# The delta-rule block's first part: mask ahead of the exponential, one z buffer, solver blocks on two queues, and x asked for first

## The chip, the cores and the metric

The kernel runs on one core of a Trainium2 chip. The metric is device time in microseconds (us), the median of several runs. The core's engines run side by side and meet at semaphores: TensorE (PE, matrix products), VectorE (DVE), ScalarE (ACT), GpSimd (POOL), and SyncE (SP), which here only issues DMA transfers.

## The reference: what is computed

A decoder block over 512 tokens of width 1024, float32. First a mixer (gated DeltaNet beside a short gated convolution), then a top-4-of-32 mixture of experts. The part that matters here, cut down:

```python
proj = rms_norm(x) @ w_in                       # q,k,v | z | a,b | short convolution | gates
q, k = l2_normalize(q), l2_normalize(k)         # 8 heads of 128, after a causal convolution and silu
gcum = cumsum(g)                                # log decay, g <= 0, per token and head
diff = gcum[..., :, None] - gcum[..., None, :]
decay = where(causal, exp(where(causal, diff, 0.0)), 0.0)
Lm = where(strict, (beta * k) @ k.T * decay, 0.0)
T = triangular_solve(Lm + eye, eye)             # unit lower triangular inverse
u, w = T @ (v * beta), T @ (k * beta * exp(gcum))
aqk = (q @ k.T) * decay
...                                             # a scan over chunks carries the state
o = rms_norm(o, g) * silu(z)
```

## The kernel before

Every large product is made in three float32r passes: a weight tile of 128 x 4 x 512 (one *half*, `kq` 0 or 1, four row blocks k of the eight) is loaded, ScalarE copies it to a rounded `hi`, VectorE subtracts to get `lo`, and TensorE multiplies hi x hi, hi x lo and lo x hi. All orders are written out by hand, one instruction stream for each engine, and the program is cut into blocks; at the end of a block every engine waits for all the others. Three places are touched.

**The front** (block of L189). SP asks for the convolution taps and gains (L197, three small transfers that land in `small_rows`), then x in four tiles of 128 tokens (L200, 512 KB each), then weights (L207). ScalarE sums squares (L257), VectorE scales the rows (L370), TensorE turns x (L466) into PSUM, ScalarE writes `xT_hi` (L267) and VectorE `xT_lo` (L376). VectorE makes the first weight half's `lo` (L384) before the first `xT_lo`. TensorE's first group (`group`, L482 to L484) needs `lo` of the half and four tiles of `xT_lo` before its first product.

**The first part of the delta-rule block** (block of L616, names from L590 on), for four chunks c of 128 tokens, 8 heads, in two halves g of four heads. TensorE turns k (L824), VectorE gets its squared norms (L735). The running decay `gc` comes from a product with the triangular mask `tri` (L867 to L869); its rows go to DRAM and come back broadcast over the partitions into `aqkT` (L635). VectorE subtracts `gc` per head and clips at 0 (`differences`, L741, 8 per chunk), ScalarE exponentiates (`exps`, L686), GpSimd multiplies with the causal mask (L661), and then multiplies the rows beta over norm, which came back broadcast in `LT` (L641), with that decay (L666). TensorE makes the q k and k k products of a chunk (`products`, L837; each shows as 2 records, 16 for a chunk), VectorE multiplies them into `LT` (L754) and `aqkT` (L756). The diagonal 32 x 32 blocks of `LT` go to DRAM (`blocks_out`, L627, 4 transfers per chunk) and return in one transfer as `W` (L649), one block per partition; VectorE inverts all 128 at once in 60 dependent small steps (L799 to L805), and the result goes to DRAM (L651).

Beside this runs the z projection, two groups of 192/2 = 96 products (L855 to L857): `zraw` (L621) to `zhi` on ScalarE (L691), to `zlo` on VectorE (`z_low`, L746), to TensorE, and its output through silu into `zT` (`z_out`, L697). TensorE's order is

```python
                products(0)
                z(0, (0, 1))
                products(1)
                z(0, (2,))
                products(2)
                z(0, (3,))
                products(3)
                z(0, (4, 5, 6, 7))
                z(1, range(KD))
```

where `products(c)` waits until VectorE has read the banks of chunk c - 1 (semaphore `s_AT`, set by L756).

**The second part** (block of L928). SP brings the inverses of chunk 0 back as the diagonal of `U` (L935) once GpSimd has zeroed it (L959); GpSimd also masks `LT` into `M` (L948). TensorE turns q and v, turns U (all L1136) and multiplies (L1130); ScalarE copies between them (L988, L994, L1011, L1000).

## Time and profile before

| | us |
|---|---|
| median of 3 runs | 1955.07 (1954.26 to 1959.21) |
| the profiled execution's own time | 1953.42 |
| its span in the trace | 1951.5 |
| PE busy | 1837.3 (94%) |
| DVE busy | 1492.9 (77%) |
| ACT busy | 1106.7 (57%) |
| POOL busy | 409.4 (21%) |
| mean granted TensorE clock | 0.969 |

The span is what the trace covers. The device time of the same execution is 1.9 us longer; the rest lies before the first and after the last instruction. All positions below are us from the span's start. The front is 0 to about 20, the first part of the delta-rule block 293.5 to 386.4, its second part follows to about 480, and the experts fill the rest. PE's busy time counts overlapping matmuls, so the distance from start to start is what one costs.

### The profile page before, as it was taken

The page shows a single profiled execution, that of the slowest core. Times are in us where ns is not written, and L with a number is a line of the kernel's source. Part 1 is how long each engine was busy: PE and PEld are TensorE (multiplying, and loading weights), DVE is VectorE, ACT ScalarE, POOL GpSimd, SP SyncE. Part 2 cuts the span into 40 slices and gives each one's busy share as a digit, 9 for nine tenths or more (in the row PEclk, how much of TensorE's full clock was granted, in tenths as well). Part 3 has the DMA queues.
Part 4 walks back from the last instruction along what each step waited for, and adds up shares of the span by engine and source line. Part 5 has one row for each costly group of instructions (what it writes and reads, how often), then busy time and mean ns, then how long its engine had stood idle before and what let it go on. Part 6 is the DMA issues. An engine that isn't in the chain of part 4 may idle for free.

```text
span 1951.5 us, 24205 instructions
## 1 busy us (share of the span) xinstructions
PE 1837.3 (94%) x8612; PEld 1529.0 (78%) x8612; DVE 1492.9 (77%) x1107; ACT 1106.7 (57%) x890; POOL 409.4 (21%) x337
## 2 busy tenths in 40 slices
PE   7999997897999985899999999999999999999995
PEld 6888875796888874688888888888888888888883
DVE  4336567657233546889999999999999999999996
ACT  4123443243241232677777777777777777777772
POOL 0000006052000010532132222322322223223231
PEclk9999997998999986999999999999999999999998
DMA  4322225102562244879999999999999999999985
GB/s 154 108 87 86 86 87 179 30 10 77 204 237 87 87 146 180 314 297 373 383 353 384 378 354 383 358 374 384 347 382 371 360 384 356 373 381 347 382 321 231
DMA packets 129070, 508.06 MB, mean 260 GB/s; under 512 B 25572, under 2 KB 25764, under 8 KB 94917
## 3 DMA queue, kind: packets, MB, share of 16 engines
q1 hardware_dynamic: 119780, 490.96, 66.0%
q0 software_dynamic: 9248, 16.54, 2.3%
q8 instruction: 28, 0.46, 0.1%
...
## 4 chain that ended last, share of the span: by engine, by line
PE 56%; DMA 1%; POOL 1%; DVE 1%; issue 1%; ACT 1%; SPq 0%; POOLq 0%; ACTq 0%; DVEq 0%
PE PM L2118 12%; PE PM L2117 12%; PE PM L2120 12%; PE PM L2136 6%; PE PM L2137 6%; PE PM L2139 6%; PE PM L2097 2%; PE PM L2111 2%; PE PM L2103 1%; DMA xg<-xn_scratch,now 1%; DMA mraw<-expert_rows_scratch 1%; DVE zT L2065 0%; POOL put_back L1923 0%; DVE zT L2073 0%; POOL by_weight L1921 0%
## 5 line engine op out<-in xcount | busy, mean ns | idle before, releaser
L1624 DVE TENSOR_TENSOR mlo<-mraw,mhi 128x2048 fp32r<-128x2048 f32 x384 | 907.5, 2397 | 60.1 <-ACT mhi L1620 58.4
L1620 ACT ACTIVATE mhi<-mraw 128x2048 fp32r<-128x2048 f32 x384 | 721.9, 1914 | 115.7 <-PE PM L2120 112.6
L2117 PE MATMUL PM<-mhi,xgT_hi 128*128 128x512 f32 x1024 | 403.3, 394 | 0.0
L2118 PE MATMUL PM<-mlo,xgT_hi 128*128 128x512 f32 x1024 | 400.5, 391 | 0.0
L2120 PE MATMUL PM<-mhi,xgT_lo 128*128 128x512 f32 x1024 | 273.9, 389 | 0.0
L2117 PEld LDWEIGHTS PM<-mhi,xgT_hi 128*128 128x128 f32 x1024 | 193.3, 189 | 40.1
L2118 PEld LDWEIGHTS PM<-mlo,xgT_hi 128*128 128x128 f32 x1024 | 193.2, 189 | 39.9
L2120 PEld LDWEIGHTS PM<-mhi,xgT_lo 128*128 128x128 f32 x1024 | 192.3, 188 | 40.5
L2136 PE MATMUL PM<-mhi,hT_hi 128*128 128x512 f32 x512 | 202.7, 396 | 1.1 <-DVE hT_lo L2034 1.1
L2137 PE MATMUL PM<-mlo,hT_hi 128*128 128x512 f32 x512 | 199.9, 390 | 0.0
L1895 POOL TENSOR_TENSOR glu<-glu 128x1024 f32<-128x1024 f32 x32 | 76.6, 2394 | 551.0 <-DVE glu L2029 551.0
L2139 PE MATMUL PM<-mhi,hT_lo 128*128 128x512 f32 x512 | 158.2, 390 | 0.0
L384 DVE TENSOR_TENSOR lo<-raw,hi 128x2048 fp32r<-128x2048 f32 x24 | 55.0, 2292 | 123.1 <-ACT hi L275 123.1
L482 PE MATMUL PS<-xT_hi,hi 128*128 128x512 f32 x352 | 137.9, 392 | 3.7 <-DVE xT_lo L376 2.7
L1402 DVE TENSOR_TENSOR lo<-qkvT,hi 128x2048 fp32r<-128x2048 f32 x20 | 45.8, 2292 | 124.8 <-ACT hi L1339 124.8
L483 PE MATMUL PS<-xT_lo,hi 128*128 128x512 f32 x352 | 137.7, 391 | 0.0
L484 PE MATMUL PS<-xT_hi,lo 128*128 128x512 f32 x352 | 137.4, 390 | 0.0
L275 ACT ACTIVATE hi<-raw 128x2048 fp32r<-128x2048 f32 x24 | 46.0, 1916 | 121.2 <-PE PS L484 120.7
L2136 PEld LDWEIGHTS PM<-mhi,hT_hi 128*128 128x128 f32 x512 | 96.5, 188 | 20.4 <-issue 1.5
L2139 PEld LDWEIGHTS PM<-mhi,hT_lo 128*128 128x128 f32 x512 | 96.4, 188 | 20.3
L1339 ACT ACTIVATE hi<-qkvT 128x2048 fp32r<-128x2048 f32 x20 | 38.2, 1913 | 130.4 <-PE PS L1499 123.9
L2137 PEld LDWEIGHTS PM<-mlo,hT_hi 128*128 128x128 f32 x512 | 96.5, 189 | 19.0
(331 smaller groups left out, 2623.6 us busy)
## 6 DMA issues: line engine op xcount, KB each, us to landing
mraw<-in_w_gate_up_dram SPq DMA_DIRECT2D x256, 1024.0 KB, 8.2
mraw<-in_w_down_dram SPq DMA_DIRECT2D x128, 1024.0 KB, 7.7
raw<-in_w_in_dram SPq DMA_DIRECT2D x24, 1024.0 KB, 5.1
qkvT<-in_w_in_dram SPq DMA_DIRECT2D x8, 1024.0 KB, 6.4
...
mraw<-expert_rows_scratch SPq DMA_DIRECT2D x6, 1024.0 KB, 12.1
zraw<-in_w_in_dram SPq DMA_DIRECT2D x4, 1024.0 KB, 6.2
qkvT<-in_w_o_gdn_dram SPq DMA_DIRECT2D x4, 1024.0 KB, 5.7
```

The costliest lines, as they stand in the source:

```text
L482: pe.matmul(dst, w_hi, xT_hi[:, k, :], start=(k == 0), stop=False)
L483: pe.matmul(dst, w_hi, xT_lo[:, k, :], start=False, stop=False)
L484: mm = pe.matmul(dst, w_lo, xT_hi[:, k, :], start=False, stop=(k == KD - 1))
L1620: nc.scalar.activation(mhi[:, split_slot(m), :], mraw[:, raw_slot(m), :], ACT.Copy).then_inc(e_h, 1)
L1624: nc.vector.tensor_tensor(mlo[:, split_slot(m), :], mraw[:, raw_slot(m), :], mhi[:, split_slot(m), :].bitcast(F32), ALU.subtract).then_inc ...
L1895: nc.gpsimd.tensor_tensor(hid, up, sig, ALU.mult).then_inc(s_hid, 1)
L2117: pe.matmul(gate_up_bank[:, n, :], xgT_hi[:, k, :], w_hi[:, n, :], start=False, stop=False)
L2118: pe.matmul(gate_up_bank[:, n, :], xgT_hi[:, k, :], w_lo[:, n, :], start=False, stop=False)
L2120: mm = pe.matmul(gate_up_bank[:, n, :], xgT_lo[:, k, :], w_hi[:, n, :], start=False, stop=(k == KD - 1))
L2136: pe.matmul(y_bank[:, n, :], hT_hi[:, k, :], w_hi[:, kk, n, :], start=(k == 0), stop=False)
L2137: pe.matmul(y_bank[:, n, :], hT_hi[:, k, :], w_lo[:, kk, n, :], start=False, stop=False)
L2139: mm = pe.matmul(y_bank[:, n, :], hT_lo[:, k, :], w_hi[:, kk, n, :], start=False, stop=(k == KD - 1))
```

## The change

In the front, the first two tiles of x are asked for ahead of the small transfers; VectorE makes four tiles of `xT_lo` ahead of the first `lo`; TensorE's first group does its hi passes of the first half (32 products) as soon as `hi` and those four tiles are there, and its lo passes (16) behind them.

In the first part of the delta-rule block: the causal mask is applied by GpSimd ahead of the exponential, as a select that puts -1e30 where the mask is off, on the rows as they come from DRAM; the subtraction of `gc` becomes the bias of the exponential, so that ScalarE runs it per head (32 instead of 8 instructions), with `ngc` = -`gc` from a new small VectorE instruction; VectorE's `differences` are gone, and the product of the beta rows with the decay moves from GpSimd to VectorE (`decayed_gates`). `zraw` has one half instead of two, so a load of z weights waits for the `zlo` of the half before it. One k block of z comes ahead of `products(0)`, and the first z split (ScalarE's copy) moves up. The last `zlo` moves from VectorE, in the middle of the inversion, to GpSimd. Blocks go out on SP's and ScalarE's queues, two each for a chunk, and come in per chunk. The inverses go out in two transfers (32 and 96 partitions), and those of chunks 0 and 1 are brought into `U` before the block ends, `U` being zeroed at its start.

```diff
+        for t in range(2):
+            sp.dma_start(x_rows[:, t, :], x_d[:, t, :]).then_inc(s_x[t], 16)
         n = 0
         for src, rows in ((gdn_conv_w[0].rearrange("j (c p) -> (j c) p", p=P), CONV * QKV),
                           (sconv_w[0].rearrange("j (c p) -> (j c) p", p=P), SCONV * KD),
                           (norm_mix_g[0].rearrange("(c p) -> c p", p=P), KD)):
             sp.dma_start(small_rows[n:n + rows, :], src).then_inc(s_rows, 16)
             n += rows
-        for t in range(TT):
+        for t in range(2, TT):
...
+        turned(range(GT))
         split(0, [0])
-        turned(range(KD))
+        turned(range(GT, KD))
...
-            for kq in range(2):
+            first = isinstance(g, int) and g == 0
+            if first:
+                pe.wait_ge(s_h, 1)
+                pe.wait_ge(s_xl, GT)
+                for k in range(GT):
+                    for j in range(GT):
+                        w_hi = hi[:, 0, k, j * P:(j + 1) * P]
+                        pe.matmul(PS[:, j, :], w_hi, xT_hi[:, k, :], start=(k == 0), stop=False)
+                        pe.matmul(PS[:, j, :], w_hi, xT_lo[:, k, :], start=False, stop=False)
+                pe.wait_ge(s_l, 1)
+                for k in range(GT):
+                    for j in range(GT):
+                        mm = pe.matmul(PS[:, j, :], lo[:, 0, k, j * P:(j + 1) * P], xT_hi[:, k, :],
+                                       start=False, stop=False)
+                mm.then_inc(s_used, 1)
+            for kq in range(1 if first else 0, 2):
                 pe.wait_ge(s_l, 2 * g + kq + 1)
                 for kk in range(GT):
                     k = GT * kq + kk
-                    if isinstance(g, int) and g == 0:
-
-                        pe.wait_ge(s_xl, max(k + 1, GT))
+                    if first:
+                        pe.wait_ge(s_xl, k + 1)
...
+FAR_BELOW = -1e30
...
+U = p2_sb("U", [P, 2, HEADS, P])
...
-zraw = pa_sb("zraw", [P, 2, GT, GW])
+zraw = pa_sb("zraw", [P, GT, GW])
...
+def blocks_out(eng, c, bs):
+    eng.wait_ge(s_LT, 2 * c + 2)
+    for b in bs:
+        rows = slice(b * BLK, (b + 1) * BLK)
+        eng.dma_start(blocks_of(nb_d, c)[b], LT[rows, c, :, rows]).then_inc(s_nb[c], 16)
+
+def blocks_in(eng, c):
+    eng.wait_ge(s_nb[c], 16 * QB)
+    eng.dma_start(W[of_chunk(c)].rearrange("p j i -> p (j i)"), nb_d[of_chunk(c)]).then_inc(s_W, 16)
+
+def inverses_in(eng, c, bs):
+    for b in bs:
+        rows = slice(b * BLK, (b + 1) * BLK)
+        eng.dma_start(U[rows, c, :, rows], blocks_of(ub_d, c)[b]).then_inc(s_uin[c], 16)
...
+            wait(sp, z_l, 2 * zg + kq)
+            sp.dma_start(zraw[:], Z_SOURCES[zg][:, kq * GT:(kq + 1) * GT, :]).then_inc(s_zraw, 16)
...
-        load_z(0, 1)
...
-        load_z(1, 0)
-        blocks_out(0)
+        load_z(0, 1)
+        for c in CHUNKS:
+            blocks_out(sp, c, (0, 1))
+            if c >= 1:
+                blocks_in(sp, c - 1)
+            if c == 2:
+                load_z(1, 0)
+        blocks_in(sp, LAST)
         load_z(1, 1)
-        for c in range(1, TT):
-            blocks_out(c)
-        sp.wait_ge(s_nb, 16 * QB * TT)
-        sp.dma_start(W[:].rearrange("p j i -> p (j i)"), nb_d).then_inc(s_W, 16)
         sp.wait_ge(s_solved, 1)
-        sp.dma_start(ub_d, W[:].rearrange("p j i -> p (j i)")).then_inc(s_ub, 16)
+        sp.dma_start(ub_d[of_chunk(0)], W[of_chunk(0)].rearrange("p j i -> p (j i)")).then_inc(s_ub, 16)
+        sp.wait_ge(s_uz, 2)
         sp.wait_ge(s_ub, 16)
+        inverses_in(sp, 0, (0, 1))
+        sp.wait_ge(s_ubr, 16)
+        inverses_in(sp, 1, range(QB))
+        for c in range(2):
+            sp.wait_ge(s_uin[c], 16 * QB)
...
+        for c in range(2):
+            nc.gpsimd.memset(U[:, c], 0.0).then_inc(s_uz, 1)
         for c in CHUNKS:
             for g in BOTH:
-                pool.wait_ge(s_exp, 2 * c + g + 1)
-                nc.gpsimd.tensor_tensor(half(aqkT[:, c], g), half(aqkT[:, c], g), each(tri[:]),
-                                        ALU.mult).then_inc(s_tri, 1)
-            for g in BOTH:
-                pool.wait_ge(s_bin[c], 16)
-                pool.wait_ge(s_tri, 2 * c + g + 1)
-                nc.gpsimd.tensor_tensor(half(LT[:, c], g), half(LT[:, c], g), half(aqkT[:, c], g),
-                                        ALU.mult).then_inc(s_decL, 1)
+                pool.wait_ge(s_gin[c], 16)
+                nc.gpsimd.affine_select(out=half(aqkT[:, c], g), in_=half(aqkT[:, c], g), compare_op=ALU.is_ge,
+                                        fill=FAR_BELOW, base=0, pattern=[[0, HS], [1, P]], channel_multiplier=-1
+                                        ).then_inc(s_tri, 1)
         pool.wait_ge(s_redk, 2 * TT + 1)
         pool.wait_ge(s_ones, 2)
         nc.gpsimd.tensor_tensor(rk, ssk, minus_half[:], ALU.pow).then_inc(s_rk, 1)
+        pool.wait_ge(z_h, 4)
+        nc.gpsimd.tensor_tensor(zlo[:, 1, :, :], zraw[:], zhi[:, 1, :, :].bitcast(F32), ALU.subtract).then_inc(z_l, 1)
...
         def exps(c):
             for g in BOTH:
-                act.wait_ge(s_diff, HEADS * c + HS * g + HS)
-                nc.scalar.activation(half(aqkT[:, c], g), half(aqkT[:, c], g), ACT.Exp).then_inc(s_exp, 1)
+                act.wait_ge(s_tri, 2 * c + g + 1)
+                for h in range(HS * g, HS * (g + 1)):
+                    n = c * HEADS + h
+                    ins = nc.scalar.activation(aqkT[:, c, h, :], aqkT[:, c, h, :], ACT.Exp, bias=ngc[:, n:n + 1])
+                ins.then_inc(s_exp, 1)
...
+        z_hi(0, 0)
         squares(2)
         squares(3)
         by_token(2)
-        z_hi(0, 0)
-        act.wait_ge(s_gc, 3)
+        act.wait_ge(s_gc, 4)
         nc.scalar.activation(eg, gc, ACT.Exp).then_inc(s_small, 1)
         nc.scalar.activation(egl, egl, ACT.Exp).then_inc(s_small, 1)
         nc.scalar.activation(ekd, ekd, ACT.Exp).then_inc(s_small, 1)
-        exps(0)
-        exps(1)
-        z_hi(0, 1)
-        exps(2)
-        exps(3)
+        for c in CHUNKS:
+            exps(c)
+        for c in CHUNKS:
+            blocks_out(act, c, (2, 3))
+            if c == 0:
+                z_hi(0, 1)
         z_hi(1, 0)
         z_out(0)
         z_hi(1, 1)
+        act.wait_ge(s_solved, 1)
+        act.dma_start(ub_d[HB:], W[HB:].rearrange("p j i -> p (j i)")).then_inc(s_ubr, 16)
+        act.wait_ge(s_uz, 2)
+        act.wait_ge(s_ub, 16)
+        inverses_in(act, 0, (2, 3))
...
-        def differences(c):
-            dve.wait_ge(s_gin[c], 16)
-            for h in range(HEADS):
-                row = aqkT[:, c, h, :]
-                nc.vector.tensor_scalar(row, row, gc[:, c * HEADS + h:c * HEADS + h + 1], 0.0, ALU.subtract,
-                                        ALU.min).then_inc(s_diff, 1)
+        def decayed_gates(c):
+            dve.wait_ge(s_bin[c], 16)
+            for g in BOTH:
+                dve.wait_ge(s_exp, 2 * c + g + 1)
+                nc.vector.tensor_tensor(half(LT[:, c], g), half(LT[:, c], g), half(aqkT[:, c], g),
+                                        ALU.mult).then_inc(s_decL, 1)
...
+        nc.vector.tensor_scalar(ngc, PB[:, 7, 0, 0:TH], -1.0, None, ALU.mult).then_inc(s_gc, 1)
...
-        dve.wait_ge(s_gc, 3)
-        differences(0)
         dve.wait_ge(s_browT, 1)
         nc.vector.tensor_copy(row_sb[:, 1, :], PB[0:TH, 0, 0, :]).then_inc(s_brs, 1)
-        differences(1)
         z_low(0, 0)
-        differences(2)
-        differences(3)
-        products(0)
-        z_low(0, 1)
-        products(1)
-        products(2)
+        for c in CHUNKS:
+            decayed_gates(c)
+            products(c)
+            if c == 1:
+                z_low(0, 1)
         z_low(1, 0)
-        products(3)
         dve.wait_ge(s_brow, 1)
         dve.wait_ge(s_small, 3)
         nc.vector.scalar_tensor_tensor(out=ebk, in0=brow, scalar=-1.0, in1=eg, op0=ALU.mult,
                                        op1=ALU.mult).then_inc(s_brk, 1)
-        dve.wait_ge(s_W, 16)
+        dve.wait_ge(s_W, 16 * TT)
...
-                z_low(1, 1)
...
+        z(0, (0,))
         products(0)
-        z(0, (0, 1))
+        z(0, (1,))
...
-        for c in CHUNKS:
+        for c in range(2, TT):
...
-        clear(0)
         masks(0)
-        clear(1)
```

How TensorE's order moves in the first part of the delta-rule block (L875 and L920 turn the beta rows; L837 and L882 are `products`; L855 to L857 and L900 to L902 are z). Before:

```order
L875 MATMUL PB<-ident,by_tok 32x128
L837 MATMUL PB<-qkvT 128x256 x8
L855 MATMUL PB<-xT_hi,zhi 128x512
L856 MATMUL PB<-xT_lo,zhi 128x512
L857 MATMUL PB<-xT_hi,zlo 128x512
```

With the change:

```order
L920 MATMUL PB<-ident,by_tok 32x128
L900 MATMUL PB<-xT_hi,zhi 128x512
L901 MATMUL PB<-xT_lo,zhi 128x512
L902 MATMUL PB<-xT_hi,zlo 128x512
L900 MATMUL PB<-xT_hi,zhi 128x512
```

The twelve products of one k block of z stand between the turned beta rows and `products(0)` now; before, 24 stood between `products(0)` and `products(1)`, and now there are twelve.

VectorE's order from the row `brow` (beta over norm) on, through the first two chunks. Before:

```order
L778 SCALAR_TENSOR_TENSOR by_tok<-by_tok 128x32
L741 TENSOR_SCALAR aqkT<-aqkT,by_tok 128x128 x8
L783 COPY row_sb<-PB 32x128
L741 TENSOR_SCALAR aqkT<-aqkT,by_tok 128x128 x8
L746 TENSOR_TENSOR zlo<-zraw,zhi 128x2048
L741 TENSOR_SCALAR aqkT<-aqkT,by_tok 128x128 x16
L754 TENSOR_TENSOR LT<-PB,LT 128x512
L756 TENSOR_TENSOR aqkT<-PB,aqkT 128x512
```

With the change:

```order
L829 SCALAR_TENSOR_TENSOR by_tok<-by_tok 128x32
L832 COPY row_sb<-PB 32x128
L796 TENSOR_TENSOR zlo<-zraw,zhi 128x2048
L791 TENSOR_TENSOR LT<-LT,aqkT 128x512 x2
L804 TENSOR_TENSOR LT<-PB,LT 128x512
L806 TENSOR_TENSOR aqkT<-PB,aqkT 128x512
```

The 32 differences have left VectorE, the copy of the beta rows stands eight instructions earlier, and two products LT x decay stand ahead of each chunk's four products with PSUM.

GpSimd's order in the same block. Before:

```order
L661 TENSOR_TENSOR aqkT<-aqkT,tri 128x512 x2
L666 TENSOR_TENSOR LT<-LT,aqkT 128x512 x2
L661 TENSOR_TENSOR aqkT<-aqkT,tri 128x512 x2
L666 TENSOR_TENSOR LT<-LT,aqkT 128x512 x2
L670 TENSOR_TENSOR by_tok<-by_tok,minus_half 128x32
```

With the change:

```order
L700 MEMSET U 128x1024 x2
L704 AFFINE_SELECT aqkT<-aqkT 128x512 x8
L709 TENSOR_TENSOR by_tok<-by_tok,minus_half 128x32
L711 TENSOR_TENSOR zlo<-zraw,zhi 128x2048
L985 UNCONDITIONAL_BRANCH
```

Sixteen two-input products have become eight one-input selects, and the last `zlo` comes behind the power (L670, now L709).

## Rows read from the trace of the kernel before

**Rows 1.** The page: busy us by engine.
```profile
PE 1837.3 (94%) x8612; PEld 1529.0 (78%) x8612; DVE 1492.9 (77%) x1107; ACT 1106.7 (57%) x890; POOL 409.4 (21%) x337
```

**Rows 2.** Timeline, front: start, us, engine, line, operation, count [idle before, releaser].
```profile
0.80 0.40 SPq L197 DMA_DIRECT2D qkvT<-in_gdn_conv_w_dram  x1
...
2.04 1.78 SPq L200 DMA_DIRECT2D qkvT<-in_x_dram  x4
...
5.36 1.06 ACT L257 ACTIVATE qkvT<-qkvT 128x1024 f32<-128x1024 f32 x1 [3.29 <-DMA qkvT<-in_x_dram]
...
16.06 4.73 ACT L267 ACTIVATE xT_hi<-PS,cols 128x512 fp32r<-128x512 f32 x8 [1.69 <-PE PS L466]
...
19.66 0.71 PE L482 MATMUL PS<-xT_hi,hi 128*128 128x512 f32 x1 [2.67 <-DVE xT_lo L376]
```

**Rows 3.** Timeline of POOL, first part of the delta-rule block, and one front row.
```profile
2.83 0.29 POOL L233 TENSOR_SCALAR_AFFINE_SELECT tri<-tri 128x128 f32<-128x128 f32 x1
...
313.90 2.58 POOL L666 TENSOR_TENSOR LT<-LT,aqkT 128x512 f32<-128x512 f32 x2 [0.29 <-DMA LT<-beta_rows_scratch]
...
326.28 1.26 POOL L661 TENSOR_TENSOR aqkT<-aqkT,tri 128x512 f32<-128x512 f32 x1
...
329.77 4.54 POOL L666 TENSOR_TENSOR LT<-LT,aqkT 128x512 f32<-128x512 f32 x2
334.27 5.46 POOL L670 TENSOR_TENSOR by_tok<-by_tok,minus_half 128x32 f32<-128x32 f32 x1
```

**Rows 4.** Timeline of DVE, same block.
```profile
305.62 1.66 DVE L741 TENSOR_SCALAR aqkT<-aqkT,by_tok 128x128 f32<-128x128 f32 x8 [0.35 <-DMA aqkT<-decay_rows_scratch]
307.19 0.27 DVE L783 COPY row_sb<-PB 32x128 f32<-32x128 f32 x1
...
311.16 16.65 DVE L741 TENSOR_SCALAR aqkT<-aqkT,by_tok 128x128 f32<-128x128 f32 x16
...
330.13 3.05 DVE L746 TENSOR_TENSOR zlo<-zraw,zhi 128x2048 fp32r<-128x2048 f32 x1
...
356.44 0.09 DVE L799 MEMSET W<- 128x32 f32 x1 [5.59 <-DMA W<-blocks_scratch]
...
363.18 2.29 DVE L746 TENSOR_TENSOR zlo<-zraw,zhi 128x2048 fp32r<-128x2048 f32 x1
```

**Rows 5.** Timeline of PE, same block.
```profile
307.61 6.48 PE L837 MATMUL PB<-qkvT 128*128 128x256 f32 x16 [2.00 <-DVE row_sb L783]
...
329.06 6.01 PE L837 MATMUL PB<-qkvT 128*128 128x256 f32 x16 [9.49 <-DVE aqkT L756]
```

**Rows 6.** Timeline of PE, same block, later.
```profile
337.68 3.61 PE L837 MATMUL PB<-qkvT 128*128 128x256 f32 x16
```

**Rows 7.** Windows: length, busy of PE, PEld, DVE, ACT, POOL, granted clock, DMA, GB/s.
```profile
329.00:334.20 5.20, 5.14 (x13) 4.19 (x14) 5.20 (x6) 0.00 (x0) 5.20 (x3) 0.54 0.17 25
...
360.60:384.30 23.70, 23.63 (x96) 19.07 (x96) 18.64 (x49) 1.68 (x2) 0.00 (x0) 0.93 0.06 23
```

**Rows 8.** DMA issues, 285 to 400: KB each, median us to landing.
```profile
zraw<-in_w_in_dram SPq DMA_DIRECT2D x4, 1024.0 KB, 6.2
...
W<-blocks_scratch SPq DMA_DIRECT2D x1, 512.0 KB, 3.2
inverses_scratch<-W SPq DMA_DIRECT2D x1, 512.0 KB, 2.7
U<-inverses_scratch SPq DMA_DIRECT2D x8, 32.0 KB, 1.9
```

**Rows 9.** Timeline of all engines where the block ends and the next begins.
```profile
380.90 0.34 SPq L651 DMA_DIRECT2D inverses_scratch<-W  x1
...
384.29 2.06 ACT L697 ACTIVATE zT<-PB 128x512 f32<-128x512 f32 x4 [22.02 <-PE PB L857]
...
391.33 1.59 PE L1136 MATMUL PB<-ident,U 128*128 128x128 f32 x8 [2.74 <-DMA U<-inverses_scratch]
...
393.45 2.17 ACT L1011 ACTIVATE vb<-PB,by_tok 128x128 f32<-128x128 f32 x8
```

37 lines of the change are left out of this document (16 added, 21 removed).

## The prediction

> **What bounds the kernel now.** I read the page first: PE is busy 94% of the span [rows 1]. So a microsecond is won only where PE stands idle or runs at the lower clock, and I looked for those places with the waits of PE, then with the timelines of the stretches around them. Three lie inside the change: the front, the first part of the delta-rule block (293.5 to 386.4), and the first microseconds of its second part. Everything behind shifts as a whole: the expert part waits for its own data and not for a fixed time.
>
> The front [rows 2]: the first square starts at 5.36, when x lands, and x was asked for at 2.04, behind three small transfers that began at 0.80. PE's first weight product comes at 19.66, released by the fourth xT_lo, whose chain is held by the turned x (xT_hi waits 1.69 for PE).
>
> The delta-rule block [rows 3 to 5]: PE makes the products of chunk 0 (307.61), then z, and then stands 9.49 us until VectorE has read chunk 0 (329.06). The reader is to see why VectorE is late. Eight differences take 1.66 while GpSimd is quiet, sixteen take 16.65 while GpSimd multiplies masks and gates [rows 4]: 0.2 against 1.04 us each. And for VectorE's zlo at 330.13, 3.05 us instead of 2.29, GpSimd's pair at 329.77 takes 4.54 instead of 2 x 1.26 [rows 3, 4]. When PE resumes, chunk 1 costs 6.01 against 3.61 for a later chunk [rows 5, 6], and the granted clock of 329.0 to 334.2 is 0.54 [rows 7]: the lower level, 1.2 GHz, after an idle PE.
>
> **Part by part.** I give times on the axis of the old trace, and add the front at the end.
>
> *Front.* x is asked for 1.24 us earlier (2.04 - 0.80). The first squares follow it; the taps now arrive behind two x tiles, but are needed only when the first variance is, after the first square. The weight half lands in the same order as before and ScalarE, which splits it, had been free for 1.69 us when the turned x came. VectorE's lo, 2.29 us, would have stood in the way of an xT_lo that starts earlier; it now comes behind four of them, and PE has 32 hi products meanwhile. A product of 128x512 takes 0.229 us from start to start at the full clock (23.63 / 96, times the mean clock of 0.93 [rows 7]), so that is over 7 us: cover enough. I take -1.1 us; bounds 0 (the weights turn out to hold it) and -1.24.
>
> *Beta rows.* The copy at 307.19 [rows 4] stood behind eight differences (1.66). These go; against that ScalarE's first z split (about 1.9 us) now precedes the last squares and delays the norms by about 1. I put the copy at 306.4. LT of chunk 0 was there at 313.90, 6.7 us after the copy [rows 3]: now about 313.1. VectorE's first zlo runs 306.7 to 309.0, and up to one select later, so PE starts z at 309.5 instead of products at 307.61: **+1.9**.
>
> *Selects and exponentials.* A select of 128x128 takes 0.29 us on GpSimd [rows 3]. The new ones have four times the columns: between 0.3 and 4 x 0.29 = 1.2 us; I take 1.2, as the memory has to be passed. Eight from 305.6, when aqkT of chunk 0 is there [rows 4], are done by 315 to 317. ScalarE's 32 exponentials with a bias per head I price by its per-head copies, 8 in 2.17 us [rows 9]: 2.2 per chunk, 8.7 in all, done by about 318. The first chunk is needed at 313, the last at about 332. Both are covered; the cover is gone when a select costs over about 3 us.
>
> *VectorE.* A product of 128x512 costs a quarter of 2.29, about 0.6 [rows 4]. Per chunk there are two with the decay and four with PSUM, 3.6 us; with two zlo that is 19 us against 4 x (3.61 + 12 x 0.229) = 25.4 us of PE between 309.5 and the end of chunk 3. The 32 differences, some 20 us (16.65 and twice 1.66), are off the engine. Chunk 0's rows are read by about 319.5, when PE is still in its second k block of z, so the 9.49 us wait goes, and with it the second start at the lower clock, 6.01 - 3.61 = 2.40. What is late next is nothing on this stretch: PE itself is. The first start at the lower clock stays as it was (6.48 for 16 records against 3.61).
>
> PE sum: -9.49 - 2.40 + 1.9 = **-10.0**. z's last silu ended at 384.29 + 2.06 = 386.35 [rows 9]; it would end at 376.35. PE's wait for the first z_out, with the lower clock behind it (0.93 in 360.6 to 384.3 [rows 7]), stays.
>
> *The inversion.* PE ends chunk 3 at 309.5 + 25.4 + 2.9 (start at the lower clock) = 337.8. Then 0.7 for LT, 0.9 for two issues, 1.9 to land, 3.2 for W at most, which was one transfer four times as large [rows 8]: solve start about 343.9 instead of 356.44. SP and ScalarE each issue two of the four now, and the z split behind ScalarE's last issues ends at about 341, its zlo at 343, so this is no later. With one zraw a load takes 6.2 us [rows 8] from its request: the third is asked for at about 333, the fourth at 343, and they are wanted at 339 and 349: just covered.
>
> The inversion lasted 380.90 - 356.44 = 24.5 us [rows 4, 9]. The zlo leaves it, -2.29. But GpSimd now runs that zlo of 128x2048 beside it, 4 x 1.26 = 5.1 us. What does VectorE pay? From both sides: 33% while they overlap (3.05 against 2.29), 1.7 us; or all 5.1. I take 5.1, because rows 3 and 4 fit whole-instruction blocking: VectorE's zlo was asked at 330.13, GpSimd's first product would end at 331.03, and 331.03 - 330.13 + 2.29 = 3.2 against 3.05; GpSimd's second then starts at 333.2, ends 334.4, and 334.31 is measured. The SBUF page of the Trainium skill (Who interferes with whom) says the same against this edit: a VectorE instruction with two SBUF inputs and a GpSimd instruction that reads SBUF exclude each other for the whole length of the first. By that rule the block ends at 377.7, by sharing at 376.35, where z holds it.
>
> So the inversion ends at 343.9 + 24.5 - 2.3 + 5.1 = 371.2. The inverses go out (2.7 at most for 96 partitions), SP issues four loads for chunk 1 (1.8), the last lands after 1.9 [rows 8]: +6.5, 377.7. That is 1.35 behind z. The block ends there: 386.35 - 377.7 = **-8.65**.
>
> *Second part.* U is there when it starts. PE's 2.74 us wait for it goes [rows 9], and the eight turned tiles behind it, 1.59 us at the lower clock, run at the full one, -0.55: **-3.3** together. The masks that GpSimd makes first (1.26 each [rows 3]) no longer stand behind the zeroing of U. Bounds -2.0 and -4.5.
>
> Sum: -1.1 - 8.65 - 3.3 = -13.05. Against the profiled execution's 1953.42 that gives 1940.4; the median of the runs is 1.65 higher, 1955.07, and gives **1942.0**.
>
> **The rivals.** *A: the new order of z on PE is hit by late neighbours.* LT is a broadcast of 512 KB per chunk that shares the queue with a z load, the power (5.46 us on GpSimd [rows 3]) now stands beside the second chunk's gates on VectorE, and the fourth z load may land late. For it: the blocking seen above; against: PE has 2.7 us of z between any two chunks. A wait of 2 us with a new start at the lower clock (2.4) costs 4.4: 1946.4. Chance 0.18.
>
> *B: more is won.* GpSimd's zlo costs the inversion little, the start of z is not held by a select, and the second part gains 4.5 as its whole first round runs at the full clock: -1.35 - 0.5 - 1.2: 1939.0. For it: PE has nothing to wait for there any more. Against: after the turned U ScalarE has eight per-head copies (2.17 us [rows 9]) in the chain, at whatever clock PE runs. Chance 0.22.
>
> *C: the gain is lost behind the inversion.* The solve chain starts no earlier than some transfer allows: the last z half or W lands 5 us late, or the z split on GpSimd runs at twice its price (the pair at 329.77 took nearly that [rows 3]), 10 us, and holds the last half of z on PE. GpSimd can start it at 351.6 (z's first group ends at 347.6, the silu and the split take 4.0) and would end at 361.6, about when PE reaches that half (48 products, 12 us, behind the wait for the silu at 350), so only the inversion pays, 5 us more: 1947.0; with transfers late as well it comes within 0.3% of no change (1949.2 or more). Chance 0.12.
>
> *D: slower.* One mechanism: the select with its two-dimensional pattern over four heads is slow on GpSimd. It is first in each chunk's chain (select, exponential, gate, product). Up to about 3.1 us each nothing is felt; the eighth is needed at about 331, after 25 us. Beyond, each microsecond costs eight. At 4.8 us each the 13 us are gone, at 6 us it is 10 us slower than before: 1965. For it: 128x512 with this pattern is not in the trace; against: 0.29 us for a quarter of it. Chance 0.03.
>
> *E: the change doesn't do what it says,* since z on PE alone holds the block: then the idle PE time would have to be filled by something else. The 9.49 us is a true stand of PE behind one named semaphore, so I give it 0.02, at 1953.
>
> **How the numbers follow.** The sum as worked out has 0.43, B 0.22, A 0.18, C 0.12, D 0.03, E 0.02. The likeliest's own bounds: front 1.2 us up or down to -1.24, copy and z start 1.5 either way, inversion path 3, second part 1.3. I let the range reach over A and B: 1935 to 1949, which leaves out most of C's tail, D and E. A measurement can tell about 0.3%, 5.9 us: faster is below 1949.2. Faster: all of the sum, A and B and half of C, 0.88; within 0.3%: 0.08; slower: 0.04.
>
> **What would show it.** In the new trace: the first weight product at about 18.5; no PE wait of more than 1 us between 309 and 337 (after the front's shift, 1.1 less each), and a granted clock of 1.0 from about 315 on; VectorE's first memset of W near 343; a VectorE wait of about 5 us inside the inversion, beside GpSimd's zlo; the last z product 10 to 11 us earlier; no U wait in the second part. The sum is wrong if the select takes over 3 us, if PE stops at the second or fourth half of z, or if the block's last act is not the return of the inverses or z's silu.

## The result and the profile after

| | before | changed |
|---|---|---|
| median of 5 runs each | 1956.86 (1954.26 to 1959.40) | 1940.77 (1937.69 to 1944.97) |
| the profiled execution's own time | 1953.42 | 1942.97 |
| its span | 1951.5 | 1941.0 |
| mean granted TensorE clock | 0.969 | 0.973 |

The ratio of the times is 0.9923, with a 95% interval of [0.991, 0.9936]; ratios below are given in the same way. The changed kernel is 0.8% faster, and the median is 1.2 us below the 1942.0 predicted. A later set of runs of the same kernel gave 0.9927 [0.9915, 0.994] (below, e12).

The page by engine answers to [rows 1]:

```profile
PE 1830.4 (94%) x8612; PEld 1523.6 (78%) x8612; DVE 1479.1 (76%) x1083; ACT 1111.3 (57%) x914; POOL 390.6 (20%) x330
```

VectorE has 24 instructions less, ScalarE 24 more. PE's busy time fell by 6.9 us with the same count. Inside the first part of the delta-rule block it is 74.7 before and 68.8 now, for 299 records each: fewer matmuls ran at the lower clock there. The total is no measure of the block, though: e3 (below), whose block is the old one, also shows 1831.7.

The waits of PE (line waited for: total, times, longest):

```profile
PE PS L463 <- DMA qkvT<-in_norm_mix_g_dram: 7.0, 1, 7.0
...
PE PB L920 <- DVE by_tok L829: 5.1, 1, 5.1
...
PE PB L1177 <- PEq L656: 3.7, 1, 3.7
...
PE PB L900 <- DVE zlo L796: 2.6, 1, 2.6
...
PE PB L900 <- ACT zT L741: 2.2, 1, 2.2
```

The 9.49 us behind VectorE's products [rows 5] is gone from the list. Inside the block there are now 5.1 for the beta rows and 2.6 for the first zlo, ahead of z, where the kernel before had 2.2 for the beta rows and 2.0 for their copy; at the end of the block 3.7 behind the return of the inverses. (In e12, a second trace of the changed kernel, the first of these is 2.5 and the last 2.4.)

VectorE through the block (timeline: start, us, engine, line, operation [idle before, releaser]), against [rows 4]:

```profile
304.89 0.28 DVE L832 COPY row_sb<-PB 32x128 f32<-32x128 f32 x1 [0.49 <-PE PB L920]
305.10 2.27 DVE L796 TENSOR_TENSOR zlo<-zraw,zhi 128x2048 fp32r<-128x2048 f32 x1
...
311.69 1.29 DVE L791 TENSOR_TENSOR LT<-LT,aqkT 128x512 f32<-128x512 f32 x2 [4.32 <-DMA LT<-beta_rows_scratch]
...
341.34 0.09 DVE L845 MEMSET W<- 128x32 f32 x1
...
350.76 4.71 DVE L849 TENSOR_TENSOR wprod<-W 128x238 f32<-128x238 f32 x1
...
355.50 0.41 DVE L851 TENSOR_TENSOR W<-W,wprod 128x238 f32<-128x238 f32 x1
```

And GpSimd, against [rows 3]:

```profile
303.73 7.07 POOL L704 TENSOR_SCALAR_AFFINE_SELECT aqkT<-aqkT 128x512 f32<-128x512 f32 x8 [9.25 <-DMA aqkT<-decay_rows_scratch]
310.77 5.46 POOL L709 TENSOR_TENSOR by_tok<-by_tok,minus_half 128x32 f32<-128x32 f32 x1
350.42 4.78 POOL L711 TENSOR_TENSOR zlo<-zraw,zhi 128x2048 fp32r<-128x2048 f32 x1 [34.19 <-ACT zhi L735]
```

GpSimd's work on the rows is over after 7 us, where it had gone on from 309 to 334. One step of the inversion takes 4.71 instead of about 0.4 us; it starts 0.34 behind the start of GpSimd's 4.78 and ends 0.27 behind its end.

Windows (length, busy of PE, PEld, DVE, ACT, POOL, granted clock, DMA, GB/s), against [rows 7]: the first 5.5 us of z, the rest of the block, and the first 4 us of the second part:

```profile
307.40:312.90 5.50, 5.48 (x13) 4.32 (x14) 1.21 (x2) 5.02 (x19) 5.50 (x7) 0.50 0.80 255
312.90:371.20 58.30, 56.05 (x245) 45.81 (x243) 42.89 (x88) 11.10 (x16) 8.11 (x2) 1.00 0.33 94
374.90:378.90 4.00, 3.97 (x23) 4.00 (x24) 1.37 (x2) 1.22 (x3) 3.99 (x4) 0.60 0.01 4
```

One start at the lower level (1.2 GHz), then 58 us of full clock (2.4 GHz) with PE busy for 56 of them. In e12 those 58 us are not all at the full level, as the part on the prediction shows.

To compare kernels I take a few landmarks from each trace, all but the first two relative to the block's start (GpSimd's memset of ones, 293.52 before): the first memset of W (solve start), the inversion's length, the end of z's last silu, GpSimd's first instruction of the second part, with which PE begins too (block end), ScalarE's first copy of turned U, and the first copy of `vnew`, some 17 us into the second part.

| | first weight product | block's start | solve start | inversion | silu end | block end | U copy | vnew |
|---|---|---|---|---|---|---|---|---|
| before | 19.66 | 293.52 | 62.92 | 24.46 | 92.83 | 93.10 | 98.59 | 115.98 |
| changed | 18.59 | 292.43 | 48.91 | 26.55 | 80.90 | 82.48 | 86.44 | 103.26 |
| e12 (changed, again) | 17.34 | 289.58 | 48.47 | 26.50 | 82.01 | 82.30 | 84.73 | 101.54 |
| e1 | 20.11 | 293.94 | 49.24 | 24.48 | 77.19 | 77.47 | 83.19 | 100.38 |
| e2 | 21.38 | 296.39 | 49.77 | 24.46 | 79.60 | 79.87 | 85.09 | 101.91 |
| e3 | 17.58 | 289.79 | 63.41 | 24.46 | 93.27 | 93.55 | 98.74 | 116.21 |
| e4 | 18.22 | 291.82 | 48.23 | 24.47 | 81.77 | 82.06 | 84.49 | 101.32 |
| e5 | 17.79 | 290.01 | 48.83 | 26.56 | 80.82 | 81.11 | 85.38 | 102.20 |
| e6 | 18.04 | 293.06 | 46.49 | 26.51 | 80.02 | 80.32 | 82.75 | 99.56 |
| e7 | 18.50 | 292.33 | 48.36 | 26.56 | 80.49 | 80.86 | 84.96 | 101.79 |
| e8 | 18.36 | 290.58 | 48.72 | 24.46 | 78.78 | 79.07 | 81.50 | 98.32 |
| e9 | 18.17 | 293.20 | 49.13 | 24.44 | 77.10 | 77.38 | 83.07 | 100.35 |
| e10 | 18.43 | 292.05 | 46.93 | 24.47 | 76.79 | 77.08 | 81.18 | 97.99 |
| e11 | 18.95 | 292.71 | 45.48 | 24.46 | 75.34 | 75.63 | 78.06 | 94.87 |

In the profiled pair `vnew` moved from 409.50 to 395.69, 13.8 us, but the end only by 10.5. The rest is scatter of the expert part: from its first gather of tokens until the experts' rows are back from DRAM the fourteen traces take 1165.9 to 1169.4, whatever the kernel; before has the shortest, the changed kernel 1168.8. One trace is therefore worth no more than some 3 us at its end, and the landmarks tell more of a single change than one time does.

The landmarks scatter too. Three pairs of traces have the same code in this block: changed and e12, e1 and e9, e10 and e11. Their block ends differ by 0.18, 0.09 and 1.45 us, their `vnew` by 1.72, 0.03 and 3.12. Single traces that differ by less than that prove nothing by themselves.

### The profile page after: what moved, and what is told of

Same layout as the page of the kernel before. It is cut to its first block, busy times and chain, and to the rows that moved or that the text cites. A ratio compares the mean times of both kernels' runs of the same rounds, so it can differ in the third digit from the quotient of the medians.

```text
span 1941.0 us, 24208 instructions
## 1 busy us (share of the span) xinstructions
PE 1830.4 (94%) x8612; PEld 1523.6 (78%) x8612; DVE 1479.1 (76%) x1083; ACT 1111.3 (57%) x914; POOL 390.6 (20%) x330
## 4 chain that ended last, share of the span: by engine, by line
PE 57%; DMA 1%; POOL 1%; DVE 1%; issue 1%; ACT 1%; SPq 0%; POOLq 0%; ACTq 0%; DVEq 0%
PE PM L2159 12%; PE PM L2158 12%; PE PM L2161 12%; PE PM L2177 6%; PE PM L2178 6%; PE PM L2180 6%; PE PM L2138 2%; PE PM L2152 2%; PE PM L2144 1%; DMA xg<-xn_scratch,now 1%; DMA mraw<-expert_rows_scratch 1%; DVE zT L2106 0%; DVE zT L2114 0%; POOL by_weight L1962 0%; ACT glu L2047 0%
## 5 line engine op out<-in xcount | busy, mean ns | idle before, releaser
L499 PE MATMUL PS<-xT_hi,hi 128*128 128x512 f32 x336 | 130.9, 390 | 1.0 <-ACT ab L299 1.0
L500 PE MATMUL PS<-xT_lo,hi 128*128 128x512 f32 x336 | 130.8, 389 | 0.0
L501 PE MATMUL PS<-xT_hi,lo 128*128 128x512 f32 x336 | 130.7, 389 | 0.0
```

Source lines behind the costliest of these rows:

```text
L499: pe.matmul(dst, w_hi, xT_hi[:, k, :], start=(k == 0), stop=False)
L500: pe.matmul(dst, w_hi, xT_lo[:, k, :], start=False, stop=False)
L501: mm = pe.matmul(dst, w_lo, xT_hi[:, k, :], start=False, stop=(k == KD - 1))
```

## The experiments

**e1, the rows alone.** The old kernel with the select on GpSimd, the exponential with a bias and the gates on VectorE; z, queues, `U` and front as before.

```diff
-pool: aqkT *= tri ; LT *= aqkT          (after s_exp, s_bin)
+pool: affine_select(aqkT, fill=FAR_BELOW)  (after s_gin)
-act:  Exp(half(aqkT))                   +act: Exp(aqkT head, bias=ngc)
-dve:  differences(0..3)                 +dve: decayed_gates(c) ahead of products(c)
```

> The kernel before with one part of the change alone: the select ahead of the exponential, the bias on ScalarE, the decay product on VectorE. Two z buffers, the old z order, one queue, the old reload of U, the old front. Theory (the gain is the end of the exclusion between GpSimd and VectorE, and with it of PE's 9.49 us stand and of the start at the lower clock behind it): no PE wait of over 1 us between products(0) and products(3), products(0) itself about 1.7 us earlier, the block's last silu 12 to 14 us earlier than 386.35, time 1943 to 1945 against 1956.9 before. Rival (the gain needs the new z order, the second queue and the early reload): less than half of it, 1950 or more, with a PE wait before products(1).

Measured: median 1939.59 of 4 runs, 0.992 [0.9899, 0.9941]. The whole gain is there with this part alone; it is more than was expected (the last silu ends at 371.13, 15.2 us earlier, and the time lies below the 1943 to 1945). VectorE's timeline in e1:

```profile
304.64 0.28 DVE L782 COPY row_sb<-PB 32x128 f32<-32x128 f32 x1 [0.48 <-PE PB L875]
...
313.82 1.29 DVE L741 TENSOR_TENSOR LT<-LT,aqkT 128x512 f32<-128x512 f32 x2 [6.43 <-DMA LT<-beta_rows_scratch]
...
343.18 0.09 DVE L799 MEMSET W<- 128x32 f32 x1 [5.52 <-DMA W<-blocks_scratch]
```

PE's waits in e1:

```profile
PE PB L875 <- DVE by_tok L779: 3.1, 1, 3.1
...
PE PB L1136 <- PEq L617: 2.4, 1, 2.4
...
PE PB L855 <- ACT zT L697: 2.2, 1, 2.2
...
PE PB L1136 <- DMA U<-inverses_scratch: 1.6, 1, 1.6
```

The block ends at 77.5 after its start, against 93.1 before and 82.4 (mean of 82.48 and 82.30) for the whole change. So inside the block the rest of the change costs 4.9 us (e9, with the same block, ends at 77.38); by the time `vnew` is made it has given 2 to 4 of them back (no wait for U), and is 1.2 to 2.9 late. The solve starts as early (49.24) with W in one transfer and the old queues as with two queues and a transfer per chunk (48.91, 48.47).

**e2, GpSimd without its mask products.** The old kernel, its causal mask on the decay left out of the computation: GpSimd's eight products with `tri` are gone, VectorE's 32 differences stay.

```diff
-nc.gpsimd.tensor_tensor(half(aqkT[:, c], g), half(aqkT[:, c], g), each(tri[:]), ALU.mult)
```

> The kernel before without GpSimd's eight multiplications by the causal mask (left out, so the decay is not masked); everything else stays. Exclusion theory: the last sixteen differences take 3 to 7 us instead of 16.65, since GpSimd's products with the beta rows only begin when those have landed (313.9), and PE's wait before products(1) falls from 9.49 to under 2 us; the last silu is 9 to 12 us earlier. Rival (VectorE's differences are slow for another reason, such as the broadcast transfers that write aqkT and LT at the same time): they still take over 12 us.

Measured: one run, 1944.31, before at 1956.07 beside it. VectorE's timeline in e2:

```profile
308.22 1.66 DVE L737 TENSOR_SCALAR aqkT<-aqkT,by_tok 128x128 f32<-128x128 f32 x8 [1.88 <-DMA aqkT<-decay_rows_scratch]
...
313.76 5.45 DVE L737 TENSOR_SCALAR aqkT<-aqkT,by_tok 128x128 f32<-128x128 f32 x16
```

Not one instruction of VectorE changed, and sixteen differences take 5.45 instead of 16.65 us [rows 4]; PE's 9.49 is gone and the solve starts at 49.77. GpSimd's first product now comes at 316.50, so most of the sixteen have no neighbour. VectorE was slow because of GpSimd's products, as the prediction read it. With all 32 differences still on VectorE the block ends 13.2 us earlier than before (79.87 against 93.10); e1, without them, has 15.6 (1.1 of the 2.4 between them is the clock behind the silu wait, see below).

**e3, the front alone,** in the old kernel (the front's part of the diff above).

> The kernel before with the changed front alone (two x tiles asked for first, four tiles of xT_lo ahead of the first lo, the hi passes of the first half ahead of its lo passes). First weight product 1.0 to 1.2 us earlier than 19.66, the delta-rule block starts 1.0 to 1.2 us earlier than 293.5, time 1 us less, which the runs can hardly tell. Rival: the taps, late behind x, hold the variance, and nothing is won.

Measured: median 1952.38 of 10 runs, 0.9981 [0.9969, 0.9993]: 1.4 to 6.1 us, 3.7 at the middle. The first weight product comes 2.1 us earlier than before and the block starts 3.7 earlier, both more than the 1.0 to 1.2 expected. The block behind it is as before (93.55). **e9, rows and front together,** asks the same from the other side:

> The kernel before with two parts of the change: the rows part of e1 and the front part of e3. By their landmarks the two are independent, so the delta-rule block takes 77 to 78 us to its second part (as in e1; 82.5 in the changed kernel) and the start moves 1 to 2 us: 1936 to 1939, that is, equal to or 1 to 4 us faster than the whole change, whose other parts (one z buffer, z ahead of the products, two queues, early reload) would then cost more than they bring. Rival (they do bring something that one trace of e1 hid): the whole change is faster than this one by 2 us or more.

Measured: 1940.16 of 5 runs, 0.9922 [0.991, 0.9935]. Beside e1 it shows nothing for the front, whose few microseconds the intervals of both cover; beside the whole change in the same set (e12, 1939.47 of 6 runs) it shows no difference either, and it missed the 1936 to 1939 expected. The rest of the change (the order of z, one `zraw`, two queues, the early return of the inverses, the last zlo on GpSimd) brings nothing that the times can tell.

**e4, the last zlo back on VectorE.**

```diff
-pool.wait_ge(z_h, 4)
-nc.gpsimd.tensor_tensor(zlo[:, 1, :, :], zraw[:], zhi[:, 1, :, :].bitcast(F32), ALU.subtract)
+if k == 14: z_low(1, 1)     # inside the inversion
```

> The changed kernel with the last zlo back on VectorE, between steps 15 and 16 of the inversion; GpSimd's is gone. Exclusion theory: the inversion takes 24.5 us instead of 26.55 (one step no longer waits 4.3 us, 2.3 us come in for the zlo); the block then ends with z's silu, 1.3 us earlier than 374.9, and PE, idle for 2.4 instead of 3.7 us, begins the second part at the full clock: 1.3 to 2.7 us in all. Rival (the slow step was no blocking but the size of its own): it stays at 4.7 us.

Measured: one run, 1938.97. VectorE's timeline in e4:

```profile
349.91 0.41 DVE L849 TENSOR_TENSOR W<-W,wprod 128x238 f32<-128x238 f32 x1
350.36 2.29 DVE L794 TENSOR_TENSOR zlo<-zraw,zhi 128x2048 fp32r<-128x2048 f32 x1
352.56 0.40 DVE L847 TENSOR_TENSOR wprod<-W 128x240 f32<-128x240 f32 x1
```

The inversion is 24.47 long, with 2.29 of zlo inside, against 26.55 with 4.71 of standing. Moving 2.29 us of work off a busy engine cost that engine 4.3, nearly twice as much. The expected 1.3 us at the block's end did not come: it ends at 82.06 with z's silu, beside 82.48 and 82.30, because TensorE's second group of z ran at the lower clock in this trace (more on that below). So the shorter inversion shows in the inversion and not in the time.

**e5, the inverses brought in late,** as before the change.

```diff
-inverses_in(sp, 0, (0, 1)); inverses_in(sp, 1, range(QB)); waits for s_uz, s_uin
-act: inverses_in(act, 0, (2, 3))
-for c in range(2, TT):      # second part's loads of U
+for c in range(TT):
```

> The changed kernel with U brought in as before, all of it in the second part, and the first part ending without it. The block then ends with z's silu, 1.3 us earlier than 374.9, but the turned U waits again 2 to 3 us: ScalarE's first copy of the turned U 0 to 2 us later than at 378.87. So the early reload is worth 2 us at most. Rival (it carries much of the gain): 4 us or more later.

Measured: one run, 1937.1; `vnew` at 102.20, between the two traces of the whole change (103.26 and 101.54). PE has no wait for U in this trace, where 2 to 3 us were expected: its sixteen turnings ran at the lower clock for 3.16 us, the transfers could start at 371.10, as `U` had been zeroed long before, and the first U is turned at 374.38. So the early return shows no gain here, and what took the wait away is at least in part the early zeroing.

**e6, products(0) ahead of z,** with the first z split left early.

```diff
-z(0, (0,)); products(0); z(0, (1,))
+products(0); z(0, (0, 1))
```

> The changed kernel with the old order on PE: products(0) straight behind the turned beta rows, then two k blocks of z. Products(0) no longer wait for the first zlo (2.57 us): they start at about 305.2 instead of z at 307.42, and the wait before products(1) stays under 1 us. z's end 1 to 2 us earlier than 371.23; the block's end is set by the inverses, whose start may move up by as much. Rival (the z block ahead of products(0) is what covers VectorE): a PE wait of several us comes back before products(1).

Measured: one run, 1940.7. PE's timeline in e6:

```profile
305.10 0.39 PE L920 MATMUL PB<-ident,by_tok 128*32 128x128 f32 x1 [5.32 <-DVE by_tok L829]
...
305.96 6.04 PE L882 MATMUL PB<-qkvT 128*128 128x256 f32 x16 [0.47 <-DVE row_sb L832]
```

In the changed kernel the place reads:

```profile
307.42 0.79 PE L900 MATMUL PB<-xT_hi,zhi 128*128 128x512 f32 x1 [2.57 <-DVE zlo L796]
```

PE begins its long run 0.47 after it has been released by the copy of the beta rows, instead of 2.57 for the zlo, and the block ends 2.1 earlier (80.32 against 82.4). The second group of z starts 53.8 us after the block's start, against 55.6 to 56.3 in all five traces with z ahead of products(0) (changed, e12, e4, e5, e7), so this is more than scatter. The 5.3 for the beta rows stays, but such a wait is no measure by itself: with the same code it is 5.1 in one trace and 2.5 in e12. The copy of the beta rows is one: it comes 12.4 to 12.9 us after the block's start in the seven traces where ScalarE's z split stands ahead of the last squares, and 10.4 to 12.1 in the four where it stands behind them (e1, e9, e10, e11).

**e7, SP's last wait gone:** the second part no longer waits at its start until U is loaded.

```diff
-for c in range(2):
-    sp.wait_ge(s_uin[c], 16 * QB)
```

> The changed kernel without SP's last wait in the first part (for the inverses of chunks 0 and 1 to have landed; TensorE waits for them itself in the second part). The block ends with z's silu: 1.3 us earlier than 374.9; PE stands 2.4 instead of 3.7 us and starts the second part at the full clock: the first copy of the turned U 1.3 to 2.8 us earlier than 378.87.

Measured: one run, 1939.24; the block ends 0.4 behind z's silu (80.49 and 80.86) instead of 1.6, 1.5 us earlier. (In e12, whose silu ends late, that distance is 0.3 with the wait in place.) PE stood 2.61 us and then did not start at the full clock, as had been expected, but at 0.57 of it for 4 us. The U copy comes at 84.96, between the two of the whole change (86.44, 84.73).

**e8, three edits at the block's end:** e4's (one step later), e7's, and z's second group in the banks that the products have left, so that it does not wait for the first group's silu.

```diff
-dst = PB[:, 4 + j]                       -pe.wait_ge(z_bank, GT * zg)
+dst = PB[:, 4 * (1 - zg) + j]            +pe.wait_ge(s_AT, 2 * TT)
-z_out(0); z_hi(1, 1)
+z_hi(1, 1); z_out(0)
```

> The changed kernel with three steps: the last zlo on VectorE in the inversion, no wait for the inverses at the block's end, and z's second group in the four banks of the products, so that it need not wait for the first group's silu (2.25 us and a dip of the clock). z's end at about 368.5 instead of 371.23, its silu ends at 370.6 instead of 373.3, ScalarE's first copy of the turned U at 373 to 375 instead of 378.87: 4 to 5.5 us in all.

Measured: one run, 1933.26 beside 1958.78 of before; the block ends at 79.07, `vnew` at 98.32, 3 to 5 earlier than in the whole change. PE does not wait between z's groups, and z ends at 76.13, against 78.80 (changed) and 79.92 (e12).

**e10, the change with five edits:** the three of e8, e6's, and the first z split back behind `by_token(2)`. Three of them undo a part of the change (e6's, the z split, the last zlo); the banks and the missing wait are new. **e12** is the change unchanged in the same set.

> The changed kernel with five edits: products(0) ahead of z, the first z split back behind the squares, the last zlo on VectorE, no wait for the inverses at the block's end, z's second group in the products' four banks. The block to its second part takes 75 to 77 us instead of 82.5, ScalarE's first copy of the turned U comes 77.5 to 79.5 us after the block's start instead of 86.4; no clock dip between z's groups. Time 1931 to 1934. Rival (the inverses' way through DRAM sets the second part's start whatever PE does): 1936 or more.

> The changed kernel once more, on the same chip and beside the others of this call: 1939 to 1942, and landmarks within the scatter of the front (first weight product 17.8 to 18.6): delta-rule block 82 to 83 us to its second part.

Measured: e10 1932.75 of 4 runs, 0.9881 [0.9867, 0.9895]; e12 1939.47 of 6, 0.9927 [0.9915, 0.994]. The intervals do not touch: e10 is 6.7 us faster than the change and 22 faster than before (1954.95 in that set). It is the fastest of the versions run (e11, below, can't be told from it). The landmarks account for a part of that: `vnew` comes at 97.99, 3.6 us earlier than in e12 (101.54) and 5.3 earlier than in the first trace of the change (103.26). Beside e9 they differ by 2.4 at `vnew`, and the medians by 7.4. Where the rest lies is open. Some is left at the block's end. ScalarE's timeline in e10:

```profile
365.82 0.86 ACTq L654 DMA_DIRECT2D U<-inverses_scratch  x2
...
366.78 2.06 ACT L737 ACTIVATE zT<-PB 128x512 f32<-128x512 f32 x4 [16.14 <-issue]
```

and PE's:

```profile
364.51 0.40 PE L900 MATMUL PB<-xT_hi,zlo 128*128 128x512 f32 x1
...
369.15 3.26 PE L1174 MATMUL PB<-ident,qkvT 128*128 128x128 f32 x16 [4.24 <-PEq L656]
```

z is complete at 364.9, but ScalarE's silu stands behind its two transfers of the inverses and starts at 366.78; PE waits 4.24 and goes on at the lower clock, so that the U copy comes at 81.18, later than the 77.5 to 79.5 expected. A silu ahead of those transfers was not tried.

**e11, e10 with the three small transfers on ScalarE's queue,** so that they start beside x and not behind two tiles of it.

> e10 with the three small transfers (taps, gains) issued by ScalarE and all four x tiles first on SP's queue. PE's first turn of the taps comes at 4 to 5.5 us instead of about 7, the last x tile is scaled 0.5 to 1 us earlier, and the first weight product comes at 17 to 17.7 instead of 18.1 on average: up to 1 us less than e10, which the runs can hardly tell. Rival (x and weights share the bandwidth, so the last x tile lands when it did): no change.

Measured: 1934.27 of 4 runs, 0.9898 [0.9884, 0.9912], no gain over e10. PE's timeline in e11:

```profile
6.75 0.45 PE L462 MATMUL PS<-ident,qkvT 128*128 128x128 f32 x1 [6.75 <-DMA qkvT<-in_norm_mix_g_dram]
```

The taps land at 6.75, within what they do on SP's queue (5.85 in e3, 7.05 in the changed kernel), where 4 to 5.5 had been expected, so another queue does not bring them earlier. The first weight product comes at 18.95, no earlier than in e10 (18.43).

## Why the prediction was right, step by step

**The mechanism, right.** VectorE was late because of GpSimd, and PE because of VectorE. e2 shows both by removing the neighbour, and e1 shows that the rows' part of the change does it alone. The 9.49 and the second slow start went as forecast, in both traces of the change.

**The front: undersized; the price of x right, that of VectorE's order missing.** Forecast -1.1 with -1.24 as the most. The first weight product stands at 19.66, 20.11 and 21.38 in the three traces with the old front (mean 20.4) and at 17.34 to 18.59 in the ten with the change's front (mean 18.1): -2.3. The block's start moves from a mean of 294.6 to 291.5, -3.1, and e3 times it at -3.7 (1.4 to 6.1). That the profiled pair shows the -1.1 of the forecast (19.66 and 18.59) is luck.

The timeline of VectorE in the front, before:

```profile
14.40 2.29 DVE L384 TENSOR_TENSOR lo<-raw,hi 128x2048 fp32r<-128x2048 f32 x1 [0.96 <-ACT hi L275]
...
16.78 5.36 DVE L376 SCALAR_TENSOR_TENSOR xT_lo<-PS,cols,xT_hi 128x512 fp32r<-128x512 f32 x8
```

ScalarE and VectorE in e1, with the same front:

```profile
15.04 2.29 DVE L384 TENSOR_TENSOR lo<-raw,hi 128x2048 fp32r<-128x2048 f32 x1 [1.46 <-ACT hi L275]
15.13 4.74 ACT L267 ACTIVATE xT_hi<-PS,cols 128x512 fp32r<-128x512 f32 x8
...
17.25 5.35 DVE L376 SCALAR_TENSOR_TENSOR xT_lo<-PS,cols,xT_hi 128x512 fp32r<-128x512 f32 x8
```

and the changed kernel:

```profile
4.02 1.06 ACT L259 ACTIVATE qkvT<-qkvT 128x1024 f32<-128x1024 f32 x1 [1.95 <-DMA qkvT<-in_x_dram]
...
13.20 1.91 ACT L277 ACTIVATE hi<-raw 128x2048 fp32r<-128x2048 f32 x1 [1.21 <-DMA raw<-in_w_in_dram]
...
15.02 4.71 ACT L269 ACTIVATE xT_hi<-PS,cols 128x512 fp32r<-128x512 f32 x8
...
15.72 2.73 DVE L378 SCALAR_TENSOR_TENSOR xT_lo<-PS,cols,xT_hi 128x512 fp32r<-128x512 f32 x4 [2.21 <-ACT xT_hi L269]
...
18.59 0.47 PE L482 MATMUL PS<-xT_hi,hi 128*128 128x512 f32 x1 [3.66 <-DVE xT_lo L378]
```

The chain through x shifts as forecast: over all these traces the first square comes about 1.3 us earlier, the last tile of x is scaled 1.3 earlier (means 13.2 and 11.8), and `xT_hi` begins 1.3 earlier (15.8 and 14.5). The other 1.0 is VectorE's order. With the old front VectorE's `lo` was out of the way in time in one trace only, the one that the prediction was read from: `xT_lo` starts there 0.7 us behind `xT_hi` (16.78 and 16.06 [rows 2]). In e1 and e2 it starts 2.1 and 2.3 behind, since `lo` stands ahead of it; with the change it is 0.7 in every trace. The prediction named that move and gave it no price of its own. What neither sees is the landing of the weights: ScalarE's split of them starts anywhere from 11.7 to 13.2 with the change's front (12.5 to 14.4 with the old one), and where it is late, as in the changed kernel's own trace, `xT_hi` stands right behind it. That is the first bound of the forecast, 0, at work in part.

From the first weight product to the block's start there are 273.8 to 275.0 us with the old front and 272.2 to 275.0 with the new one, so the hi passes that no longer wait for `lo` may bring something beyond it, or nothing; that was not taken apart.

**The start of z: +0.9 instead of +1.9.** With the front's 1.1 taken off, the copy of the beta rows was forecast at 305.3 and came at 304.89; z was forecast at 308.4 and came at 307.42. The prediction let VectorE's zlo wait for a select. It was the select that waited. GpSimd's selects in the changed kernel (by source line; shortest, median, longest in ns):

```profile
L704 POOL TENSOR_SCALAR_AFFINE_SELECT aqkT<-aqkT x8: 629/629/2897, 303.7 to 310.2; 128x512 f32<-128x512 f32 x8
```

0.63 us each, half of the 1.2 that was taken, and one of 2.90: 0.63 and the 2.27 of the zlo that ran beside it. (By the trace that select began at 305.0, just ahead of the zlo's 305.10, and was the one that waited all the same.) Rival D, the slow select, is out. Rival A, late neighbours, did not come: from z's start to the wait for the silu at 348.69, PE waits nowhere for more than 1 us. But that z goes ahead of products(0) at all is a loss of about 2 us (e6), which the prediction carried in its +1.9 without asking what the order was worth. In e1, with neither z nor its split ahead, products(0) starts 11.1 us after the block's start, where z starts at 15.0 in the changed kernel and products(0) started at 14.1 before.

**The clock behind the silu wait: either level, by trace.** The wait of 2.2 stayed, as forecast. Behind it the granted clock was 1.00 in the changed kernel's trace, where 0.93 had been carried over from [rows 7], and 0.93 in e12's. z's second group in both:

```profile
348.69:371.23 22.54, 22.54 (x96) 17.98 (x96) 17.81 (x39) 1.65 (x1) 4.78 (x1) 1.00 0.09 24
```

```profile
345.38:369.50 24.12, 24.11 (x96) 19.14 (x96) 17.78 (x39) 1.66 (x1) 4.74 (x1) 0.93 0.13 30
```

The same 96 products take 1.6 us more. The wait is 2.25 us in all eleven traces that have it, and the clock is at the full level behind it in five (changed, e1, e5, e7, e9) and starts at the lower one in six (before, e12, e2, e3, e4, e6). As the same code gives both, one trace can't claim this for the change; whether the full level has become likelier (none of the three without the select, five of the eight with it) is open. It put the end of z's silu at 373.33 in the profiled trace against the 375.25 forecast (376.35, less the front).

**The inversion: right in kind, 0.8 less.** Forecast 27.3, measured 26.55 and 26.50: the blocked step costs 4.3 (4.71 - 0.41), not 5.1, because GpSimd's zlo is one instruction of 4.78 and began 0.3 ahead of the step. e4 settles sharing against exclusion: with sharing 1.7 would have been paid. The rule of the Trainium skill (the SBUF page, Who interferes with whom), exclusion for the whole instruction, agrees with two places where VectorE's instruction has two SBUF inputs: 4.71 beside 4.78, and the select of 2.90 beside a zlo of 2.27. The differences of e2 (16.65 against 5.45) read one tile, so the rule as the prediction quotes it does not speak of them; there e2 is the evidence. Rival B's first condition fell here.

**The solve start and the block's end: right.** Solve start forecast 50.4 after the block's start, measured 48.9 and 48.5, since z and with it the products were earlier. (The terms of that forecast add up to 344.5 and not to the 343.9 that it goes on with, 51.0 after the start; the 6.5 of the return is 6.4. Neither changes a reading.) ScalarE's timeline shows what the single `zraw` does; the first row is the last z split:

```profile
337.01 1.92 ACT L735 ACTIVATE zhi<-zraw 128x2048 fp32r<-128x2048 f32 x1 [16.04 <-DMA zraw<-in_w_in_dram]
...
371.27 2.06 ACT L741 ACTIVATE zT<-PB 128x512 f32<-128x512 f32 x4 [20.93 <-PE PB L902]
```

It waited for a load asked for at 331.15, and VectorE's zlo at 338.96 precedes the memset of W at 341.34. In e6, e10 and e11, where products come earlier, the solve starts earlier too. The return of the inverses (SP's timeline):

```profile
367.89 0.30 SPq L686 DMA_DIRECT2D inverses_scratch<-W  x1
370.30 2.79 SPq L654 DMA_DIRECT2D U<-inverses_scratch  x6
```

From 367.89 to the block's end at 374.91 are 7.0 us, forecast 6.5. That return ended the block in this trace, as forecast, with the silu 1.6 ahead; in e12 the silu was late by the lower clock and the block ended 0.3 behind it. The block gained 10.6 and 10.8 where 8.65 stood in the sum.

**The second part: the wait right, the clock not.** Forecast -3.3. From block end to `vnew` it was 22.88 before, 20.78 and 19.24 after: -2.1 and -3.6. PE's wait for U is gone in both (and in e5, where U comes late, so the zeroing ahead of time may be what removed it). The 1.5 between them is the clock of the first 4 us: 0.60 in the changed kernel's trace, 1.00 in e12's. The sum had counted on the full clock; the two traces hold both cases.

**The sum.** In the profiled pair: front -1.1, block -10.6, second part -2.1, together -13.8 at `vnew` against the -13.05 forecast, of which the expert part's scatter hid 3.3 at the end. Over all traces the front is worth 2 us more, and the timed medians differ by 16.1 and 15.5. The block gained 2 more than its term (solve start 1.5 earlier, inversion 0.8 shorter, the return 0.5 longer), the second part 1.2 less or 0.3 more; the total fell inside the range because the one large term was read from a named wait. That it came within 1.2 us of the forecast is partly luck: terms of 1 to 3 us in the front, the block and the second part were off both ways, and the clock behind two short waits of PE decides 1 to 2 us each in a single trace. Rival B (1939.0) has the sum's size but not its reasons; C and E are out with the times.
